# A scan stage of a hybrid RWKV-7 / RG-LRU layer: unmasked levels with predicated writes, products by direction, one recurrence piece per chunk, and the state's decay on ScalarE

## What is computed

```
# RWKV-7, per head (8 heads of 64), both directions, 2304 steps
sa = einsum('bhvk,bhk->bhv', s, -kk_t)
s  = s * w_t + sa (x) (kk_t * a_t) + v_t (x) k_t
y_t = einsum('bhvk,bhk->bhv', s, r_t)

# RG-LRU, 512 channels, both directions, 2304 steps
log_a = -8 * sigmoid(...) * softplus(-lam);  a = exp(log_a)
bt = sqrt(-expm1(2 * log_a)) * (ig * xc)
h_t = a_t * h_(t-1) + bt_t
```

## Time and profile before

| | us |
|---|---|
| median of 3 runs | 4158.69 (4156.33 to 4160.95) |
| the profiled execution, its own time | 4148.39 |
| its span in the trace | 4146.4 |
| busy: PE / DVE / ACT / POOL | 3638.3 / 2411.1 / 1913.3 / 1230.8 |
| mean granted TensorE clock | 0.925 of full speed |
| the scan stage | 1117 to 2366 after the start |

### The profile page before, as it was taken

One profiled execution on the slowest core, in us unless ns is written; L12 is line 12 of the kernel. 1 busy time (PEld: TensorE's weight loads), 2 busy tenths in 40 slices (PEclk: granted clock), 3 DMA queues, 4 the chain that ended last, 5 costly groups with the idle time before them and its releaser, 6 DMA issues. The chain is left out here.

```text
span 4146.4 us, 93389 instructions
## 1 busy us (share of the span) xinstructions
PE 3638.3 (88%) x39677; PEld 3171.0 (76%) x39677; DVE 2411.1 (58%) x4475; ACT 1913.3 (46%) x2991; POOL 1230.8 (30%) x1222
## 2 busy tenths in 40 slices
PE   5699999999778888888887679799399999999997
PEld 2578888888667777777776578776399999999987
DVE  3236676630057666767677655433667676766666
ACT  3246666541145555556555544233134344444364
POOL 1323333321055555555554255200101111110102
PEclk7899999999889988888889789899699999999999
DMA  5235555542355453545443357343366666676787
GB/s 171 69 119 177 183 173 172 175 139 74 100 113 121 98 113 88 114 100 101 104 105 75 115 166 241 123 142 112 103 204 204 209 209 210 205 214 193 234 286 227
DMA packets 694211, 630.21 MB, mean 152 GB/s; under 512 B 190434, under 2 KB 602916, under 8 KB 692772
## 3 DMA queue, kind: packets, MB, share of 16 engines
q1 hardware_dynamic: 644644, 512.72, 42.7%
q0 software_dynamic: 22688, 80.75, 6.6%
q10 hardware_dynamic: 26464, 30.77, 2.5%
HBM read 462.49 MB, written 161.50 MB: 150 GB/s over the span
## 5 line engine op out<-in xcount | busy, mean ns | idle before, releaser
L579 PE MATMUL moe_h<-moe_xt_hi,moe_w_hi 128*128 128x256 f32 x2048 | 582.5, 284 | 7.0 <-DVEq L58 3.4
L431 DVE TENSOR_TENSOR moe_w_lo<-moe_w_lo_whole,moe_w_hi 128x2048 fp32r<-128x2048 f32 x254 | 446.5, 1758 | 240.7 <-ACT moe_w_hi L647 195.6
L579 PE MATMUL moe_h<-moe_xt_hi,moe_w_lo 128*128 128x256 f32 x2048 | 580.2, 283 | 0.0
L579 PE MATMUL moe_h<-moe_xt_lo,moe_w_hi 128*128 128x256 f32 x2048 | 580.2, 283 | 0.0
L1968 PE MATMUL inward_pp<-u_u_hi,inward_w_hi 128*128 128x512 f32 (+1 forms) x1360 | 527.6, 388 | 20.8 <-POOL inward_w_lo L2129 20.8
L1968 PE MATMUL inward_pp<-u_u_lo,inward_w_hi 128*128 128x512 f32 (+1 forms) x1360 | 516.1, 380 | 0.0
L1968 PE MATMUL inward_pp<-u_u_hi,inward_w_lo 128*128 128x512 f32 (+1 forms) x1360 | 515.7, 379 | 0.0
L579 PEld LDWEIGHTS moe_h<-moe_xt_hi,moe_w_hi 128*128 128x128 f32 x2048 | 393.3, 192 | 18.1 <-issue 5.9
L579 PEld LDWEIGHTS moe_h<-moe_xt_lo,moe_w_hi 128*128 128x128 f32 x2048 | 393.5, 192 | 3.6
L579 PEld LDWEIGHTS moe_h<-moe_xt_hi,moe_w_lo 128*128 128x128 f32 x2048 | 393.4, 192 | 0.0
L487 POOL DMA_INDIRECT scratch_x<-moe_ys,moe_who x30 | 87.5, 2918 | 864.5 <-DVE moe_ys L753 746.2
(11 more groups left out here) (388 smaller groups left out, 9003.8 us busy)
## 6 DMA issues: line engine op xcount, KB each, us to landing
moe_w_lo_whole<-in_moe_w SPq DMA_DIRECT2D x384, 512.0 KB, 5.4
scan_by_parity<-scratch_ops SPq DMA_DIRECT2D x144, 192.0 KB, 7.4
scan_over<-scratch_ops SPq DMA_DIRECT2D x72, 384.0 KB, 7.1
inward_w_lo_whole<-in_w_in SPq DMA_DIRECT2D x38, 512.0 KB, 4.5
scan_aq<-scratch_ops SPq DMA_DIRECT2D x36, 516.0 KB, 4.8
scratch_ops<-inward_ops_bk SPq DMA_DIRECT2D x72, 256.0 KB, 2.7
scratch_ops<-inward_ops_aq SPq DMA_DIRECT2D x72, 256.0 KB, 2.7
scratch_gates<-inward_out SPq DMA_DIRECT2D x64, 256.0 KB, 2.1
```

The costliest lines, as they stand in the source:

```text
L431: return nc.vector.tensor_tensor(x_lo, x, x_hi.bitcast(F32), ALU.subtract)
L579: mm = nc.tensor.matmul(hb[ft % 2][m][:, 0:CAP], w_, x_, start=(k == 0 and part == 0), stop=(k == KD - 1 and part == 2))
```

## The change

1. **Levels.** The masked copies H and GpSimd's ten operations a window are gone. ACT now writes L with scale -1, and forward multiplies the whole L with W. The product then has values outside the level's blocks, so DVE no longer adds it: it copies it into W by predicate, where a table `chosen` (loaded from constants) marks the level's places. W has two buffers and Wf is gone.
2. **Joint products by direction.** A round is issued and signalled as two halves, d = 0 and d = 1, and DVE's masked copies run in the order d, then u. PE's waits for round 2, and for the turning of B and K, are by half too.
3. **Recurrence.** DVE runs one recur at each S (piece k-4) instead of two at the S of chunks 0 and 2. Its last part, which writes z, is now keep, run at the next X, behind series.
4. **State.** The scaling of the state goes from DVE to ACT (Identity with a per-partition scale). ACT issues at S the two copies of y first, then the four scalings, then window. X waits for the scaled state alone.
5. **GpSimd.** The two parts of add are issued after squares of chunk 0 and of chunk 2. It doesn't wait for the masks ahead of its first load.
6. **Masks.** Six masks fewer are loaded, and `chosen` by two DMAs; DVE waits for all three before its first masked copy.

```diff
@@ constants, MASKS
-        if m == 0:
-            masks.append(-both([level & b for b in before]))
-        masks.append(-both([level & b for b in before[::-1]]))
+        masks.append((-1 if m == 0 else 1) * both([level & b for b in before]))
-MASKS = ["strict", "incl", "nincl", "lev0", "lev0t", "lev1t", "lev2t", "lev3t", "lev4t", "lev5t"]
+MASKS = ["strict", "incl", "nincl", "lev0"]
@@ PE: joint
-                for u in U:
-                    if r == 1:
-                        AC[u].wait(pe, "V", it)
-                    else:
-                        DV[u].wait(pe, EVICTED[FIRST_OF[u][0]][1] + "1", it)
                 pe.wait_ge(s_over[uK], 32 * it + 32)
-                for k in range(8):
-                    mmB = beside(uB, k, ob[uB], aq[uB][:, b, :], False)
-                    mmK = beside(uK, k, over[uK], over[uK][:, 2 * G:], True)
-                PE[uB].did("B", mmB)
-                PE[uK].did("K", mmK)
+                for d in range(2):
+                    for u in U:
+                        if r == 1:
+                            AC[u].wait(pe, "LV"[d], it)
+                        else:
+                            DV[u].wait(pe, f"{EVICTED[FIRST_OF[u][0]][1]}{d}", it)
+                    for k in range(4 * d, 4 * d + 4):
+                        mmB = beside(uB, k, ob[uB], aq[uB][:, b, :], False)
+                        mmK = beside(uK, k, over[uK], over[uK][:, 2 * G:], True)
+                    PE[uB].did(f"B{d}", mmB)
+                    PE[uK].did(f"K{d}", mmK)
@@ PE: forward
-                PO[u].wait(pe, f"H{m}", it)
-                held, old = of(H[u][(m - 1) % 2]), of(W[u])
+                held, old = of(L[u]), of(W[u][b])
@@ PE: state, step X
-                        DVc[u].wait(pe, f"Sb{c - 1}", it)
-                        ACc[u].wait(pe, f"Y{c - 1}", it)
+                        ACc[u].wait(pe, f"Sb{c - 1}", it)
@@ ACT
-                    AC[u].did("L", act.activation(flat(L[u][:, :, :]), bank[u][2], ACT.Copy))
+                    AC[u].did("L", act.activation(flat(L[u][:, :, :]), bank[u][2], ACT.Copy, scale=-1.0))
+                    DVc[u].wait(act, f"Ub{c}", it)
+                    for d, at in ((0, c), (1, 3 - c)):
+                        gain = aq[u][:, a[1], 4 * G + 4 * d + at:4 * G + 4 * d + at + 1]
+                        ACc[u].did(f"S{'ab'[d]}{c}", act.activation(S[u][:, (c + 1) % 2, d, :], undecayed[u][:, d, :], ACT.Identity, scale=gain))
...
+                    for part in ("YS" if step == "S" else step):
+                        for u in U:
+                            state(u, chunk, part, c)
@@ DVE: square, state, recur
-                D.did(f"W{m}", dve.tensor_tensor(halves_of(W[u] if m < 5 else Wf[u][b]), halves_of(W[u]), gain, ALU.add))
+                where = chosen[:, m - 1].bitcast(I32).unsqueeze(1).broadcast_to([P, 2, 4, HD])
+                D.did(f"W{m}", dve.copy_predicated(halves_of(W[u][b]), where, gain))
-                    D.wait(dve, f"Ub{c}", it)
-                    for d, at in ((0, c), (1, 3 - c)):
-                        gain = aq[u][:, b, 4 * G + 4 * d + at:4 * G + 4 * d + at + 1]
-                        D.did(f"S{'ab'[d]}{c}", dve.tensor_scalar(S[u][:, (c + 1) % 2, d, :], undecayed[u][:, d, :], gain, None, ALU.mult))
                     if step == "X":
                         if k:
                             series(k - 1)
+                        if k > 4:
+                            keep(k - 5)
...
-                    elif c[0] and chunk % 2 == 0:
-                        recur(4 * (c[0] - 1) + chunk)
-                        recur(4 * (c[0] - 1) + chunk + 1)
+                    elif c[0]:
+                        recur(k - 4)
@@ POOL
-                PO[u].did(f"H{m}", pool.tensor_tensor(four(H[u][(m - 1) % 2][:, :, :]), four(L[u][:, :, :]), masked(f"lev{m}t"), ALU.mult))
-                if 2 * it < 4 * KD:
-                    for half in range(2):
-                        count = add(2 * it + half, count)
+                for chunk in range(4):
+                    squares(4 * (it - 1) + chunk)
+                    if chunk % 2 == 0 and 2 * it < 4 * KD:
+                        count = add(2 * it + chunk // 2, count)
```

More of the change, by code:

```diff
@@ L2307, in scan @@
         xp = each("by_parity", [P, 12, 2, HD])
-        W, L = (each(x, [P, 2, G]) for x in "WL")
+        L = each("L", [P, 2, G])
         FT = each("FT", [P, 2, 2 * G])
-        Wf, byB = twice("Wf"), twice_beside("tB_Lb")
+        W, byB = twice("W"), twice_beside("tB_Lb")
         aq = each("aq", [P, 2, 4 * G + 8])
-        H = [[n.sb(f"H{u}{m}", [P, 2, G]) for m in range(2)] for u in U]
         S = each("S", [P, 2, 2, HD])
@@ L2426, in reload_own @@
                     PEc[u].wait(sp, "S3", it)
[L2427 removed]
+                    ACc[u].wait(sp, "Sb3", it)
                 load(it + 2, True, False)
@@ L2439, in _ @@
             load(0, True, True)
-            sp.dma_start(masks[:, :], t["consts"][:, n_main:n_main + len(MASKS) * P]).then_inc(s_masks, 16)
+            levels_at = n_main + len(MASKS) * P
+            sp.dma_start(masks[:, :], t["consts"][:, n_main:levels_at]).then_inc(s_masks, 16)
+            levels = t["consts"][:, levels_at:levels_at + len(LEVELS) * P].rearrange("p (k f) -> p k f", f=HD)
+            for q in range(2):
+                sp.dma_start(chosen.rearrange("p m (d q) f -> p (m d) q f", q=2)[:, :, q, :], levels).then_inc(s_masks, 16)
             load(1, True, False)
@@ L2748, in states @@
                         gates(k)
-                        for j in range(NJ - 1):
-                            last = 2 * NG * (j + 1) - 1
-                            if (c[0], chunk) == (last // 4 + 1, last % 4):
-                                store_z(j)
                     elif step == "Z":
@@ L2756, in states @@
                         squares(k)
+                        for j in range(NJ - 1):
+                            if k - 4 == 2 * NG * (j + 1):
+                                store_z(j)
                     else:
@@ L2793, in _, with begin @@
         def _(dve):
-            def begin(u, r, a):
+            def begin(r, a):
                 it, b, half = a
-                D = DV[u]
-                if r in (1, 2):
-                    product = FIRST_OF[u][r - 1]
-                    PE[u].wait(dve, product, it)
-                    second = lambda x: x[u][b][:, :, :, 1, :]
-                    for name, x, part, mask in ((("W0", four(W[u][:, :, :]), 0, "lev0"), ("Lb", second(byB), 1, "nincl")) if product == "B" else
-                                                (("La", four(La[u][b][:, :, :]), 0, "strict"), ("Lk", second(byK), 1, "incl"))):
-                        for d in U:
-                            pairs = bank[u][2 + d].rearrange("p (c x f) -> p c x f", x=2, f=HD)[:, :, part, :]
-                            D.did(f"{name}{d}", dve.tensor_tensor(x[:, d], pairs, masked(mask)[:, d], ALU.mult))
+                if r not in (1, 2):
+                    return
+                second = lambda x: x[:, :, :, 1, :]
+                for d in range(2):
+                    for u in U:
+                        D, product = DV[u], FIRST_OF[u][r - 1]
+                        PE[u].wait(dve, f"{product}{d}", it)
+                        pairs = bank[u][2 + d].rearrange("p (c x f) -> p c x f", x=2, f=HD)
+                        if product == "B":
+                            D.did(f"W0{d}", dve.tensor_tensor(four(W[u][b][:, :, :])[:, d], pairs[:, :, 0, :], masked("lev0")[:, d], ALU.mult))
+                            D.did(f"Lb{d}", dve.tensor_tensor(second(byB[u][b])[:, d], pairs[:, :, 1, :], masked("nincl")[:, d], ALU.mult))
+                        else:
+                            D.did(f"La{d}", dve.tensor_tensor(four(La[u][b][:, :, :])[:, d], pairs[:, :, 0, :], masked("strict")[:, d], ALU.mult))
+                            D.did(f"Lk{d}", dve.tensor_tensor(second(byK[u][b])[:, d], pairs[:, :, 1, :], masked("incl")[:, d], ALU.mult))
             def square(u, m, a):
@@ L2964, in start_solve @@
                     DV[u].wait(pool, "W01", it)
-                    PO[u].did("W0", pool.tensor_tensor(blocks(W[u]), blocks(W[u]), units, ALU.add))
-            def level(m, it):
-                for u in U:
-                    if m == 1:
-                        AC[u].wait(pool, "L", it)
-                        if it:
-                            PE[u].wait(pool, "F5", it - 1)
-                    elif m == 2:
-                        if it:
-                            PE[u].wait(pool, "F4", it - 1)
-                    else:
-                        PE[u].wait(pool, f"F{m - 2}", it)
-                    PO[u].did(f"H{m}", pool.tensor_tensor(four(H[u][(m - 1) % 2][:, :, :]), four(L[u][:, :, :]), masked(f"lev{m}t"), ALU.mult))
+                    own = blocks(W[u][it % 2])
+                    PO[u].did("W0", pool.tensor_tensor(own, own, units, ALU.add))
             def squares(k):
```

63 lines of the change are left out of this document (25 added, 38 removed).

## The result

The change takes 4048.49 us (median of 4 runs, 4039.63 to 4056.7) beside 4157.8 for the kernel before (4 runs, 4156.33 to 4160.95): a ratio of 0.9736, 95% interval 0.9712 to 0.976. The forecast was 4046 in a range of 3995 to 4115, so time and side were right. Two further measurements of the same kernel gave 4031.4 and 4038.2; its time moves by up to 17 us from one measurement to the next, its ratio from 0.9685 to 0.9736.

The account below looks back on a forecast made before the run. No engine was full; a chain from engine to engine along PE's order bound the window. 47 us work, 7.65 idle and 5.1 lower clock made 59.8 against 66.3; seventeen windows -111, with ends -113: median 4046, range 3995 to 4115.

Parts of the forecast that it names:

- Joint rounds: PE's 2.42 us stop ahead of joint round 2 vanishes; a new wait of 0.35 for half 1 appears.
- State on ACT: Each scaling on ACT takes 0.31 us; PE's stop at Z of chunk 1 grows from 0.27 to 2.35.
- slower case: Rival, chance 0.06: ACT's window starts over 2.7 us later at each chunk, eating the gain; at 3.5 later, 4210 us.
- Recurrence: PE's waits for Z's copy (2.9 us a window) and at level 4 (2.0) go; level 5's grows from 1.1 to 2.0.
- Predicated writes: A predicated copy on DVE takes 0.72 us, +0.04 on two exposed levels, 0.1 us a window in all.
- add beside recur: GpSimd's add parts beside recur and series stretch five instructions by 0.2 us each, 1 us, within slack.
- rival at 4136: DVE loses about 0.8 us on each of five instructions beside each add part, giving 4136 us; chance 0.06.
- Loads: aq lands in time, no term; `chosen` DMAs and GpSimd's earlier 512 KB load cost 0 to 4 us, taken as 2.
- Ends: First window gains 2.42 us, last some 2, extra loads cost 2: -2 in sum beside the seventeen windows' -111.
- Clock: Long PE stops fall from three to two a window, so the lower clock costs 5.1 us instead of 7.7.
- the clock doesn't come back: Rival, chance 0.12: PE's two remaining stops keep all 7.7 us of lower clock; -4.0 a window, 4091 us.
- small operations are dear: Rival, chance 0.11: ACT scalings at 0.60 us and predicated writes at 0.90 leave 0.7 a window, 4145 us; half-way 4095.

Follow-up runs that it names:

- e5: The change with joint rounds whole again, the halves signalled only at the seventh and eighth of eight pairs and waits asking for the later half: 4075.2 us.
- e3: The change with the scaling of the state back on DVE and X waiting for y again: 4055.5 us, beside 4031.4 for the change.
- e4: The change with the recurrence pieces in pairs again at chunks 0 and 2, keep behind each: 4057.2 us.
- e6: The change with ten 128x512 mask multiplications a window put back on GpSimd, into tiles nobody reads: 4085.0 us.
- e1: The change with GpSimd's two add parts and their loads back at the end of its list: 4028.6 us.
- e2: The change with the additions in place but only the first of the 32 loads of w_mod issued: 4017.7 us.
- c1: The change measured again without any edit, as the base of e1 to e3: 4031.4 us.
- c2: The change measured once more without any edit, as the base of e8 and e10: 4038.2 us.
- e8: The change with SP's loads of over waiting for the forward products of level 3: 4021.9 us.
- e10: The change with the second and fourth recurrence pieces moved behind the writes of levels 1 and 4: 4036.5 us.

## Why the prediction was right

The sum went by one window: 47 us of work at full clock, 7.65 idle, 5.1 for the lower clock, 59.8 together. Measured: 47 + 9.2 + 4.2 (51.2 busy less 47) = 60.4. The profiled execution was to take 4035 and took 4039.6. The median is 2.5 us off, less than the kernel's own time moves between measurements, and partly by luck: errors of both signs met, as the last points of this list show.

- *Joint rounds*: forecast 2.42 to nothing. It is 0.47, a stop of 0.26 and one of 0.22 at the halves. The 0.35 ahead of the turning of K did not come. DVE's start and its 1.37 us for four copies were right; e5 gives the part 2.4 us a window in the time.
- *State on ACT*: 0.31 forecast, 0.333 measured. The stop at Z was to be 2.35 and is 2.05, sixteen times. The slower case, window starting over 2.7 us later at every chunk, did not occur: in the window around 1750 the step window starts 1.8 us behind y's start, 2.9 at chunk 0, against 0.85 before, and without ACT's scaling the kernel is 24 us slower (e3).
- *Recurrence*: the stop of S for Z's copy went (2.9), and that at level 4 (2.0), as forecast; level 5 waits 1.54 instead of 2.0. The forecast put this down to the split first. By e4 and e6 the split or the missing masks would each have done for Z's copy. In time e6 costs some 46 us, and e4 nothing that can be told.
- *Predicated writes*: 0.72 forecast, 0.725 measured. The 1.04 ns for each element more is what the kernel before shows between the masked copies of 256 elements (line 2805, median 415 ns) and the additions of 512 (681).
- *add beside recur*: 1 us within slack. Right: e1's time shows no difference, and DVE's instructions lose 1.5 us a window beside the additions. The rival at 4136, in the chances under "port" (0.06), is out in its size: it needed 8 us a window, and the scan's median stays 751 ns with the additions beside it, its maximum 1319. The additions do stretch DVE's instructions, at a fifth of the rival's price, and the multiplications of e6 do by 0.76 us for each. That a port is the cause was the author's explanation, and no run shows it.
- *Loads*: this is the term that was missing. The step "GpSimd's earlier 512 KB load, at a place where PE waits for loads, cost 0 to 4" looked at the first load alone. In every window with additions that load now meets SP's reload, and the packets that bring PE's instructions come late behind both. The "issue" stops grew by 42 us in sixteen windows, 2.6 each, which is 1.1 more than all of the idle that was missed (9.2 less 7.65). e1 and e2 show that the load makes about 20 of the 42. For the rest there is only a reading: as many packets start behind full DMA engines as before (57 and 61), but more of them end in a stop (35 and 21), as they would where PE, no longer held by stops of its own, uses up its instructions faster.
- *Ends*: the first window gained 2.6 (2.42 forecast), sixteen windows 95 (104), the last work from 2252.1 on before and 2153.4 now 12.6 (8.5), and what lies outside lost 1.6 (2).
- *Clock*: two thirds of 7.7 was the forecast, 4.2 came. The reason given was long stops, from three to two; that the low clock costs in proportion to their number was the author's estimate, and no run shows it. The 7.7 itself agrees with the trace, where half of the 15.8 us a window at 0.50 is 7.9. What the runs show in place of the two thirds: of the sixteen stops of 2.1 us at Z only seven were followed by a stretch at 0.50: the windows above show one at 0.50 from 1207.6 and one at 1.00 from 1752.6. Before, 13 of the 15 stops at S, most of them 3 to 4 us, were followed by one. The shorter stops cost less than in proportion. And most of the low clock of the change stands behind stops that the sum did not have. Put down to the last stop over 0.8 us that ended within 4 us before it, 31 of the 119.5 us at 0.50 in sixteen windows follow the stop at Z, none the one at level 5, and 82 follow "issue" stops, as here:

```profile
1391.82:1394.17 2.35, 0.00 (x0) 0.00 (x0) 1.84 (x3) 1.89 (x6) 0.65 (x2) 1.00 1.27 171
1395.31:1398.72 3.41, 3.41 (x58) 3.02 (x55) 1.32 (x4) 1.29 (x4) 0.00 (x0) 0.50 1.22 257
```

c1 and c2 say the same (41 and 31 us behind Z, 10 and 10 behind the waits for W, 96 and 89 behind "issue"). So the two stops that the forecast priced at 5.1 us a window cost about 1 (half of 31/16), and the missing term brought some 2.6 (half of 82/16). That the clock's term came out near its size is luck, and the missing term cost about twice its 2.6 us of idle time.

Of the rivals, "the clock doesn't come back", "small operations are dear" and "the wait only moves" fell with the granted clock of 0.94 (single low stretches last 3.4 to 13.7 us before and 3.4 to 10.2 in the change), the 333 and 725 ns, and the idle time of 9.2.

## What to carry to other kernels

An instruction off the critical path can be the dearest of a stage: ten multiplications a window on GpSimd, for which PE hardly ever waited, cost some 46 us when they were put back with their results unused, through the stretch of VectorE's instructions and through the work that queued behind them on GpSimd. Find the stretch by the spread between median and maximum of a line, and count the removed work there, not at the waits of TensorE. When a sum takes stops away from TensorE, look at what its DMAs do in the same place: its own instructions come by DMA too, a packet of 16 KB for some 255 of them here, and late packets put "issue" stops where the others were. Check such a stop against the packets of the instruction queue before looking for another cause. And mend stops in order of what the clock makes of them: removing 1 us at level 5 gave nothing; doing it together with a cut of the 2 us stop at Z and e1's edit gave 1%.

## What the hardware did that was not expected

- PE stood for up to 5.0 us in the middle of like matmuls whose operands were all there, in 17 of the 21 cases of 1.5 us and more at a DMA share of 0.92 or above. In all 14 traces these stops (471 of 473) end 1.2 to 2.0 us after a packet of 16,384 bytes has landed on the instruction queue. These stops went from 64 to 41 us when GpSimd's loads of 512 KB were moved with their additions (c1 to e1), and from 65 to 55 when SP's loads of over were delayed (c2 to e8).
- A stop of 2.1 us at one and the same place was followed by a granted clock of 0.50 in 7 of 16 cases; which ones, no row of this case tells.
- GpSimd's multiplications of 128x512 cost VectorE 0.76 us of work each in e6 and some 0.55 in the kernel before (against e3); its additions of 128x256, some 15 a window, cost it 1.5 us a window in all.
- Loads that had landed just in time became a stop as soon as PE was quicker elsewhere: aq 4.1 to 12.2 us (c2 to e10), with the same median of 4.8 us from issue to landing in e10 as in the earlier trace rows.
